# Side-by-side high and low weights in the narrow products of a four-layer kernel

## The reference

```python
# layer 1: 64 columns, the rotary part of the keys
h = x @ w_in                      # mla_w_in: 512 + 512 + 64 + 2048 columns
k_pe = h[..., o2:o3]              # o3 - o2 = MLA_ROPE = 64
# layer 2: 8 columns, input and forget gates of 4 heads
EV_SIZES = (W_A, W_A, W_A, W_A, W_B, W_B, W_B, W_B, W_B, 2 * H_B)
# layer 3: 16 columns, decay and beta gates of 8 heads
OD_SIZES = (W_C, W_C, W_D, W_D, W_D, W_D, H_D, H_D)
```

## Time and profile before

| | |
|---|---|
| median of 3 executions | 2509.97 |
| lowest, highest | 2507.91, 2510.02 |
| the profiled execution: time | 2509.25 |
| the profiled execution: span | 2507.5 |
| its mean granted clock of TensorE | 0.991 |
| TensorE busy | 2451.6 (98%) |
| VectorE busy | 1390.0 (55%) |
| ScalarE busy | 1219.7 (49%) |
| DMA | 414.50 MB, mean 165 GB/s |

### The profile page before, as it was taken

The page is one execution under the profiler, slowest core; times in us unless marked ns, Lnnn a source line. Parts: engine busy times, 40 slices in busy tenths (PEclk is TensorE's granted clock), DMA queues, the critical chain, the costliest instruction groups (busy, mean ns, idle before and its releaser), DMA issues.

```text
span 2507.5 us, 30431 instructions
## 1 busy us (share of the span) xinstructions
PE 2451.6 (98%) x12222; PEld 2063.7 (82%) x12222; DVE 1390.0 (55%) x1857; ACT 1219.7 (49%) x1651; POOL 124.7 (5%) x127
## 2 busy tenths in 40 slices
PE   8999999999999999989999979999999999999999
PEld 6888888888888888868898868888888887888887
DVE  5646464546464646555556665555455566746554
ACT  4444444444444545445555455555444468644443
POOL 1101010101010101000000000000000000000000
PEclk9999999999999999989999989999999999999999
DMA  7555454555455554535554555555555555433344
GB/s 237 185 168 184 153 189 163 185 167 180 162 180 168 168 183 163 206 122 191 168 137 134 186 157 174 181 184 173 181 168 168 170 186 168 134 101 118 101 134 134
DMA packets 367136, 414.50 MB, mean 165 GB/s; under 512 B 27722, under 2 KB 298276, under 8 KB 366484
## 3 DMA queue, kind: packets, MB, share of 16 engines
q1 hardware_dynamic: 365588, 405.63, 50.7%
q0 software_dynamic: 1408, 6.94, 0.8%
HBM read 410.42 MB, written 2.10 MB: 165 GB/s over the span
## 4 chain that ended last, share of the span: by engine, by line
PE 91%; DVE 4%; ACT 3%; issue 1%; DMA 1%; SPq 0%; POOL 0%; DVEq 0%; ACTq 0%
PE ps L566 25%; PE ps L568 25%; PE ps L567 25%; PE ps L1001 2%; PE ps L608 2%; PE ps L729 1%; ACT whi L1127 1%; DVE wlo L1692 1%; PE ps L716 1%; PE ps L721 1%; PE ps L775 1%; PE ps L776 1%; PE ps L777 1%; PE ps L713 0%; DVE x L1799 0%
## 5 line engine op out<-in xcount | busy, mean ns | idle before, releaser
L1692 DVE TENSOR_TENSOR wlo<-raw,whi 128x1024 fp32r<-128x1024 f32 (+1 forms) x774 | 949.1, 1232 | 832.6 <-ACT whi L1127 829.4
L566 PE MATMUL ps<-whi,xh 128*128 128x512 f32 x2944 | 1177.2, 400 | 7.5 <-DVE wlo L1692 7.5
L1127 ACT CAST whi<-raw 128x1024 fp32r<-128x1024 f32 (+1 forms) x774 | 801.2, 1040 | 765.1 <-PE ps L568 756.8
L568 PE MATMUL ps<-whi,xl 128*128 128x512 f32 x2944 | 1150.4, 391 | 0.0
L567 PE MATMUL ps<-wlo,xh 128*128 128x512 f32 x2944 | 1148.3, 390 | 0.0
L566 PEld LDWEIGHTS ps<-whi,xh 128*128 128x128 f32 x2944 | 554.6, 188 | 117.2 <-issue 7.2
L568 PEld LDWEIGHTS ps<-whi,xl 128*128 128x128 f32 x2944 | 553.5, 188 | 118.1
L567 PEld LDWEIGHTS ps<-wlo,xh 128*128 128x128 f32 x2944 | 555.0, 189 | 108.3
L2432 POOL TENSOR_TENSOR work<-work 128x512 f32<-128x512 f32 x48 | 77.2, 1608 | 874.5 <-DVE work L1885 488.5
L1213 ACT ACTIVATE work<-work,small 128x128 f32<-128x128 f32 (+1 forms) x80 | 46.1, 577 | 153.0 <-DVE small L1810 153.0
L1001 PEld LDWEIGHTS ps<-work 128*128 128x128 f32 x544 | 67.7, 191 | 6.1 <-DVE work L2280 2.6
(11 more groups left out here) (374 smaller groups left out, 1569.4 us busy)
## 6 DMA issues: line engine op xcount, KB each, us to landing
raw<-in_dsa_w_in SPq DMA_DIRECT2D x320, 512.0 KB, 4.5
raw<-in_ev_w_in SPq DMA_DIRECT2D x144, 512.0 KB, 4.5
raw<-in_od_w_in SPq DMA_DIRECT2D x96, 512.0 KB, 4.6
raw<-in_mla_w_in SPq DMA_DIRECT2D x48, 512.0 KB, 4.3
raw<-in_dsa_w_out SPq DMA_DIRECT2D x32, 512.0 KB, 4.6
raw<-in_mla_w_out SPq DMA_DIRECT2D x32, 512.0 KB, 4.7
raw<-in_ev_w_out SPq DMA_DIRECT2D x32, 512.0 KB, 4.7
raw<-in_od_w_out SPq DMA_DIRECT2D x32, 512.0 KB, 4.6
```

The lines of the kernel that those rows point to most:

```text
L566: pe.matmul(o, xh[:, k, tokens[tb]], hi, start=start and s + l == 0, stop=False)
L568: m = pe.matmul(o, xl[:, k, tokens[tb]], hi, start=False, stop=stop and s + l == 2)
L1127: act.copy(whole_half(whi[:, h % 4], widths[u]), whole_half(raw[:, u % 4, 2 * (h % 2):2 * (h % 2) + 2], widths[u])).then_inc(hi_done, 1)
L1692: dve.tensor_tensor(whole_half(wlo[:, h % 4], n), whole_half(raw[:, h // 2 % 4, 2 * (h % 2):2 * (h % 2) + 2], n), whole_half(whi[:, h % 4] ...
```

## The change

High and low weights of a narrow slab stand side by side in whi: chunk t has its n high columns at 0 and its n low columns at max(n, 32). One product with xh takes both (`few_both`: 128, 40 and 48 columns wide for n = 64, 8 and 16) and leaves high x high in rows 0 to n and low x high in rows from max(n, 32) on; a second one adds high x low to rows 0 to n. That makes 32 products of a slab instead of 48. The rows of the low part are copied out by a second copy of ScalarE, and VectorE adds them to the first. In layers 2 and 3 the transposes of the gate rows wait for that add (marks rows of mg_d and dg_d) instead of ScalarE's copy.

```diff
--- before.py
+++ after.py
@@ -240,7 +240,7 @@
-        la_d = marks("la_d", "t k ms norm")
+        la_d = marks("la_d", "rows t k ms norm")
@@ -253,7 +253,7 @@
-        mg_d = marks("mg_d", "bias neg min relu lf rli rlf scan diff max e acol ecol")
+        mg_d = marks("mg_d", "rows bias neg min relu lf rli rlf scan diff max e acol ecol")
@@ -264,7 +264,7 @@
-        dg_d = marks("dg_d", "beta dt neg min relu sp gg rg dec*2 dcol")
+        dg_d = marks("dg_d", "rows beta dt neg min relu sp gg rg dec*2 dcol")
@@ -313,7 +313,7 @@
-            kr, cost, sint = c(S), c(S), c(S)
+            kr, krl, cost, sint = c(S), c(S), c(S), c(S)
@@ -334,6 +334,7 @@
+            growl = rlf
@@ -394,6 +395,7 @@
+            rlow = flat(lane[1].E)[:, S:2 * S]
@@ -458,6 +460,19 @@
         def whole_half(v, n):
 
             return v[:, :, 0:n] if n > FEW else flat(v)[:, 0:8 * n].rearrange("p (t n) -> p t n", t=8)
+
+        def low_at(n):
+
+            return max(n, 32)
+
+        def few_high(h, n):
+            return flat(whi[:, h % 4])[:, 0:16 * low_at(n)].rearrange("p (t n) -> p t n", t=8)[:, :, 0:n]
+
+        def few_low(h, n):
+            return flat(whi[:, h % 4])[:, 0:16 * low_at(n)].rearrange("p (t n) -> p t n", t=8)[:, :, low_at(n):low_at(n) + n]
+
+        def few_both(h, n):
+            return flat(whi[:, h % 4])[:, 0:16 * low_at(n)].rearrange("p (t n) -> p t n", t=8)[:, :, 0:low_at(n) + n]
 
         def last_weights(w, layer):
             for s, m in LAST_UNITS:
@@ -577,18 +592,20 @@
 
             def few_columns(side, n, bank, layer=None, between=None):
 
-                o = ps[0:n, bank, 0:S]
+
                 for s in range(2):
                     h = half[0]
                     pe.wait_ge(lo_done, h + 1)
-                    hi, lo = whole_half(whi[:, h % 4], n), whole_half(wlo[:, h % 4], n)
+                    both_, hi = few_both(h, n), few_high(h, n)
                     for t in range(8):
                         k = 8 * s + t
                         if layer is not None and k % 2 == 0:
                             pe.wait_ge(*xt_d.at(8 * layer + k // 2, "lo"))
-                        pe.matmul(o, hi[:, t], xh[:, k, :], start=k == 0, stop=False)
-                        pe.matmul(o, lo[:, t], xh[:, k, :], start=False, stop=False)
-                        m = pe.matmul(o, hi[:, t], xl[:, k, :], start=False, stop=k == KT - 1)
+                        if k:
+                            pe.matmul(ps[0:n, bank, 0:S], hi[:, t], xl[:, k, :], start=False, stop=False)
+                        m = pe.matmul(ps[0:low_at(n) + n, bank, 0:S], both_[:, t], xh[:, k, :], start=k == 0, stop=k == KT - 1)
+                        if k == 0:
+                            m = pe.matmul(ps[0:n, bank, 0:S], hi[:, t], xl[:, k, :], start=False, stop=False)
                         if t == 7:
                             m.then_inc(half_done, 1)
                         if t % 2:
@@ -898,7 +915,7 @@
                     yield from attend(h0 + hh, scores, turned, pv, 3, hh == 1)
 
             def gate_vectors():
-                pe.wait_ge(*mg_a.at(0, "rows"))
+                pe.wait_ge(*mg_d.at(0, "rows"))
                 pe.transpose(ps[:, 7, 0:8], L2.grow[0:8, 0:P], ident[0:8, 0:8])
                 pe.transpose(ps[:, 7, 8:16], L2.grow[0:8, P:S], ident[0:8, 0:8]).then_inc(*mg_p.up("cols"))
                 yield from turns(8)
@@ -1089,7 +1106,7 @@
 
             def delta_gates():
                 yield from turns(4)
-                pe.wait_ge(*dg_a.at(0, "rows"))
+                pe.wait_ge(*dg_d.at(0, "rows"))
                 pe.transpose(ps[:, Q + 1, 0:16], L3.rdec[0:16, 0:P], ident[0:16, 0:16])
                 pe.transpose(ps[:, Q + 1, 16:32], L3.rdec[0:16, P:S], ident[0:16, 0:16]).then_inc(*dg_p.up("cols"))
                 yield from turns(16)
@@ -1124,8 +1141,9 @@
                 act.wait_ge(raw_in[u % 4], loaded[u + 4])
                 if h >= 4:
                     act.wait_ge(half_done, h - 3)
-                act.copy(whole_half(whi[:, h % 4], widths[u]),
-                         whole_half(raw[:, u % 4, 2 * (h % 2):2 * (h % 2) + 2], widths[u])).then_inc(hi_done, 1)
+                n = widths[u]
+                act.copy(whi[:, h % 4, :, 0:n] if n > FEW else few_high(h, n),
+                         whole_half(raw[:, u % 4, 2 * (h % 2):2 * (h % 2) + 2], n)).then_inc(hi_done, 1)
 
             def unit(side, fine=False, then=None):
                 for s in range(2):
@@ -1354,7 +1372,8 @@
             act.copy(L1.cc[:, 0], ps[:, 0:2, :]).then_inc(*la_a.up("out0"))
             few_columns(nothing)
             act.wait_ge(half_done, half[0])
-            act.copy(L1.kr[0:64], ps[0:64, Q, 0:S]).then_inc(*la_a.up("rows"))
+            act.copy(L1.kr[0:64], ps[0:64, Q, 0:S])
+            act.copy(L1.krl[0:64], ps[64:P, Q, 0:S]).then_inc(*la_a.up("rows"))
             project(nothing)
             act.wait_ge(half_done, half[0])
             act.copy(L1.cc[:, 1], ps[:, 2:4, :]).then_inc(*la_a.up("out2"))
@@ -1466,7 +1485,8 @@
             few_columns(side)
             run(side)
             act.wait_ge(half_done, half[0])
-            act.copy(L2.grow[0:8], ps[0:8, 2, 0:S]).then_inc(*mg_a.up("rows"))
+            act.copy(L2.grow[0:8], ps[0:8, 2, 0:S])
+            act.copy(L2.growl[0:8], ps[32:40, 2, 0:S]).then_inc(*mg_a.up("rows"))
             for pair in range(4):
                 side = attention2(pair - 1) if pair else later(4, gate_vectors())
                 project(side)
@@ -1643,7 +1663,8 @@
 
             few_columns(nothing, lambda: turn_x(3, (6, 7)))
             act.wait_ge(half_done, half[0])
-            act.copy(L3.rdec[0:16], ps[0:16, Q, 0:S]).then_inc(*dg_a.up("rows"))
+            act.copy(L3.rdec[0:16], ps[0:16, Q, 0:S])
+            act.copy(L3.rlow[0:16], ps[32:48, Q, 0:S]).then_inc(*dg_a.up("rows"))
             run(squares(3))
             side = lanes(delta_gates, delta, lru, lambda n: nothing)
 
@@ -1689,8 +1710,10 @@
                     return
                 dve.wait_ge(hi_done, h + 1)
                 n = widths[h // 2]
-                dve.tensor_tensor(whole_half(wlo[:, h % 4], n), whole_half(raw[:, h // 2 % 4, 2 * (h % 2):2 * (h % 2) + 2], n),
-                                  whole_half(whi[:, h % 4], n).bitcast(F32), ALU.subtract).then_inc(lo_done, 1)
+                hi = whi[:, h % 4, :, 0:n] if n > FEW else few_high(h, n)
+                dve.tensor_tensor(wlo[:, h % 4, :, 0:n] if n > FEW else few_low(h, n),
+                                  whole_half(raw[:, h // 2 % 4, 2 * (h % 2):2 * (h % 2) + 2], n),
+                                  hi.bitcast(F32), ALU.subtract).then_inc(lo_done, 1)
 
             def unit(side, fine=False, then=None):
                 for s in range(2):
@@ -1931,6 +1954,8 @@
                 yield
                 dve.wait_ge(*la_a.at(0, "tab"))
                 dve.wait_ge(*la_a.at(0, "rows"))
+                dve.tensor_tensor(L1.kr[0:64], L1.kr[0:64], L1.krl[0:64], ALU.add).then_inc(*la_d.up("rows"))
+                dve.wait_ge(*la_d.at(0, "rows"))
                 t1, t2 = L1.t1[:, 0], L1.t2[:, 0]
                 dve.tensor_tensor(t1[0:64], L1.kr[0:64], L1.cost[0:64], ALU.mult)
                 dve.tensor_tensor(t2[0:32], L1.kr[32:64], L1.sint[32:64], ALU.mult)
@@ -2054,6 +2079,8 @@
 
             def gate_vectors():
                 f = L2.gif[:, :, 4:]
+                dve.wait_ge(*mg_a.at(0, "rows"))
+                dve.tensor_tensor(L2.grow[0:8], L2.grow[0:8], L2.growl[0:8], ALU.add).then_inc(*mg_d.up("rows"))
                 dve.wait_ge(*mg_a.at(0, "read"))
                 dve.wait_ge(l2_in[1], 16)
                 dve.tensor_tensor(L2.gif, L2.gif, bc(L2.ifb, 1, TB), ALU.add).then_inc(*mg_d.up("bias"))
@@ -2312,6 +2339,8 @@
 
             def delta_gates():
                 yield
+                dve.wait_ge(*dg_a.at(0, "rows"))
+                dve.tensor_tensor(L3.rdec[0:16], L3.rdec[0:16], L3.rlow[0:16], ALU.add).then_inc(*dg_d.up("rows"))
                 lam = vcol("lam", 8)
                 dve.tensor_scalar(L3.tmp8, lam, -1.0, None, ALU.mult).then_inc(*c3_d.up("neg"))
                 dve.wait_ge(*c3_d.at(0, "neg"))
```

## The result

The changed kernel takes 2513.15 us, the kernel before 2508.53 us, medians of 21 executions each; the ratio is 1.0018, with an interval of 1.0011 to 1.0025. That is 4.6 us more, where 4.7 were forecast: a loss of under 0.2%, but clear of zero. One execution of the changed kernel took 2989.54 us at a mean granted clock of 0.775 and is left out of the ratio.

What follows compares the result with a forecast made beforehand. TensorE, busy for 98% of the span, was taken as the bound. Terms -1.7 + 0 + 1.6 + 2.6 + 2.2 = +4.7 us on the median of 2509.97 gave 2514.7 us, range 2510.9 to 2518.0.

Steps and rivals of the forecast that it cites:

- Layer 1: Narrow slab of layer 1: 16 products fewer save 1.7 us, bounds 0.6 to 1.8.
- no gain kept: Layer 2 narrow slab: 1.8 us saved becomes a 2.3 us wait before the second half at 1488.80; saved 0.
- the new wait: Layer 2 gate-row transposes wait for VectorE's add behind three splits: +1.6 us, bounds 0.4 to 2.0.
- slab 1.2 us: Layer 3 narrow slab ends 1.2 us sooner, not shortened in full because its last chunks wait for xl.
- The stop: Layer 3 transposes wait for the add far back in VectorE's order: 3.8 us stop, +2.6 us net, bounds 2.2 to 3.2.
- The clock: Half clock behind layer 3's stop: +2.2 us, between 1.6 and 2.85; a fall in layer 3 alone had chance 0.38.
- fall behind the waits of layer 2: Rival: clock also falls in layer 2, at the wait before the second half; 1.5 us more, 2516.2 us; chance 0.27.
- given back by later waits: Rival: later layer 3 waits return up to 4.8 us of the stops, 2510 to 2511 us; chance 0.13.
- Nothing waits: Rival: 48 products go without new waits, layers 1 to 3 save 5.3 us, 2504.7 us; chance 0.03.

Runs made afterwards that it cites:

- the waits alone: Kernel before with its 48 products, VectorE operations put at the places of the adds and TensorE's transposes waiting for them: 2514.96 us, ratio 1.0025.
- the add of layer 3 early: Changed kernel with layer 3's add moved right behind the narrow slab, ahead of the scale of the norm: 2507.66 us, ratio 0.9998.
- both adds early: Changed kernel with the adds of layers 2 and 3 moved ahead in VectorE's order: 2505.89 us, ratio 0.9983.
- the add of layer 2 alone early: Changed kernel with only layer 2's add moved ahead of the splits, layer 3's add left late: 2510.40 us, ratio 1.0007.
- 2502.65 us: Changed kernel with both adds moved ahead, layer 2's bias table reversal behind the first wide slab, layer 3's sums of squares two steps later: ratio 0.9979.
- the bias table later: Changed kernel with both adds moved ahead and layer 2's bias reversal and memsets behind the first wide slab: 2508.07 us, again 2506.92 us.
- both adds early and the sums later: Changed kernel with both adds moved ahead, bias table in its old place, layer 3's sums of squares two steps later: 2505.27 us, ratio 0.9985.

## Why the prediction was right

**Layer 1**, 1.7 us: measured 5.44 - 3.73 = 1.71. The row of L775 was the right one to take. By the Trainium skill's rule on weight loads (TensorE: Matmul & The Clock Gate, section LDWEIGHTS) seen in full it would have been 0.9, an estimate. The records of the loads did grow from 134 ns (64 columns) to 188 ns (128 columns), 54 ns as by that rule, but the products still follow at 0.117 us, so the growth lies beside them.

**Layer 2**, no gain kept: in essence right, but off by 0.8 us in this profile. From the last transposes of x to the second half it took 12.48 us before and 11.67 now. The low part still waits for the bias table, but its DMA let VectorE begin 7.52 us behind those transposes (1480.11 less 1472.59) instead of 8.33. In the profile of the waits alone it was 8.27, with the add of layer 3 early 8.22, in the others less. Why it lands sooner in some executions wasn't tried. The wait before the second half was 1.00 us, not 2.3: those 0.8 us, and the narrow slab itself took 0.5 us longer than reckoned, since its first 1.4 us still ran at half the clock (until 1477.32), and before only its first 0.4 us. Such a stretch of 17.1 us at half the clock stands at the beginning of layers 1 and 2 in all twelve profiles, also of the kernel before, around a wait of 8.4 us for VectorE; the prediction's reckoning of the slab left it out.

**Layer 2**, the new wait, +1.6 us: the transposes stopped for 1.54 us, and from the second half on they came 5.94 us later instead of 4.31. Both experiments that take this wait out bear it out, within their noise: 1.8 us between the medians with one and with both adds early, and 2.75 between the changed kernel and the one with the add of layer 2 alone early.

**Layer 3**, slab 1.2 us: measured 1.18, with TensorE now waiting for xl in it (0.49 us in the row above), as was reckoned from the earlier trace rows. **The stop**, 3.8 us and +2.6 us net: measured 3.89, and 13.03 us from the beginning of the slab to the transposes instead of 10.29, +2.7. **The clock**, 2.2 us for a fall behind the stop: right in kind, too dear in size for this profile. It stayed at half for 3.42 us and cost 1.6 us by the time between the transposes and the next wait at L982 (51.26 us instead of 49.68), the lower bound. The price isn't the same each time: in the profile with the add of layer 2 alone early, behind a stop of the same length, this time is 52.36 us, 2.7 more than before. The upper bound of 2.85 was read from rows that begin late: the clock at the start of the program stood at half for 6.83 us and not 5.7, from 15.67 to 22.50.

So the terms measured sum to -1.7 - 0.8 + 1.6 + 2.7 + 1.6 = +3.4 us, and the medians differ by 4.6. Where the other 1.2 us lie isn't shown, since only one execution of each kernel was profiled and that of the changed kernel was its fastest. Half clock is the likely place: eight executions of the changed kernel lie at 2510 to 2511.3 us with a mean clock of 0.990 or 0.991, and eight at 2514 to 2517.5 us with 0.988. In the profiled pair the change gave back 0.7 us between L982 and the end. So the mechanism was right, but that 4.7 met 4.6 so closely is partly luck: the forecast had 0.8 us too much in layer 2 and 0.6 too much for the clock, and nothing for these 1.2 us. Its time of 2514.7 us also stands on the median of three executions, 2509.97; 21 gave 2508.53.

**The rivals.** The clock did not fall behind the waits of layer 2 in any of the profiles that have them. The stops were not given back by later waits: those before L982 and L1016 are 0.92 and 1.36 us in both profiles. "Nothing waits" came nearest with both adds early, but at 2505.89 us and not 2504.7, since layer 2 kept little of its gain; 2502.65 us took the bias table and the sums of layer 3 out of the way too.

## What to carry to other kernels

Before a result is passed through another engine, look at where that engine's step stands in its fixed order, not at how long it takes: an add of 0.4 us stopped TensorE for 3.9 us because it stood behind a wait for something else. Put such a step right where its input is ready. And when a saving vanishes, compare the granted clock by stretch before looking for a lost overlap.

## What the runs showed that I had not expected

In both profiles with the bias table later the clock fell about 1 us after the start of L1033 (16 products with one moving column), which had waited 1.35 us, and stayed at half for 13.7 us although TensorE was busy all the time. The same wait and the same products had no fall behind them in the kernel before. In the profile with both adds early and the sums later the fall came 1.1 us behind L1033 with no wait in the 11.9 us before it, so a wait isn't needed for it; whether the narrow products of L1033 are what brings it isn't shown, since the same rows, also without a wait, stood at full clock in the profile of 2502.65 us. The length of this stretch in the middle of layer 3 differs from profile to profile: none in three of the twelve, 3.4 us in two, 6.8 in five and 13.7 in two. It goes with the spread of the kernel before, whose executions above 2512.6 us all have a mean clock of 0.988; none of those was profiled, so where their half clock lies isn't known.
